# Weight parts, turns and sums in another order in a two-block transformer kernel on one core

## The chip, the cores and the metric

One Trainium2 chip, one of its cores. Work runs on five engines with instruction streams of their own: TensorE (PE, matrix products, with its weight loads as PEld), VectorE (DVE), ScalarE (ACT), GpSimd (POOL) and SyncE (SP); POOL and SP here mostly issue DMAs. The metric is the device time of one execution in microseconds (us), lower is better.

## The reference

Everything is fp32, batch 1, 1024 positions, width 1024, with a context of 256 rows beside them (1280 rows, ten chunks of 128).

```python
def reference(...):
    x = first_block(x, c, ctx, c_ctx, ...)     # two layers
    return second_block(x, p, positions, ...)

# first_block, layer 0: modulation from silu(c) @ w_mod, then
hx = rmsnorm(x, g_pre) * (1 + scale) + shift             # and the same of ctx
ux = hx @ ab_w_in                                        # q, k, v, o, z of 4 heads, pool, gates
qk = short_conv(...)                                     # 3 taps
h  = mlstm_chunkwise(forward) + reversed mlstm_chunkwise # 4 heads, chunks of 128, state C (256x256)
y  = [head_rmsnorm(h*o) * silu(z), multiscale_pool(u) * silu(z)] @ ab_w_out
# layer 1: window attention with context keys and a sink

# second_block
z = rms_norm(h, norm_mix) @ w_in
o_gla  = gla_mixer(...)                                  # 4 heads, chunks of 64
lam = exp(sum(lam_q1*lam_k1)) - exp(sum(lam_q2*lam_k2)) + lam_init
# diff_attention, each of 8 blocks of 128 queries and 4 heads, keys up to the block's end:
pr = softmax(where(mask, q @ k.T, -1e30))                # two maps, m = 0 and 1
o_diff = (pr[0] - lam * pr[1]) @ v
o_diff = rms_norm(o_diff, norm_g) * (1 - lam_init)
h = h + concat(o_gla, o_diff) @ w_out
h = h + (gelu(conv(rms_norm(h) @ w_up)) ...) @ w_down    # feed-forward
gate = sigmoid(rms_norm(h, norm_ple) @ w_ple_gate)
h = h + gate * (p @ w_ple_proj)
return rms_norm(h, norm_final)
```

## The kernel before, in words

The kernel is one program of hand-ordered parts that run behind each other: first stage (0 to about 67 us: modulation vectors, norm, gate product), the four recurrent heads, the pool, the output projection, layer 1, then the second block with its gated linear attention (gla), differential attention, output projection, feed-forward (up, down) and the last part (ple). There is no scheduler: each engine runs its instructions in the order in which the code issues them, and waits on semaphores for the others.

**Products in three passes.** Each fp32 operand is split into a rounded high part and a rest, and three products (high-high, high-low, low-high) are summed. Weights come by DMA into `W`; ACT copies the high part of half an item to `W_rounded` (`split_hi`, line 403) and DVE subtracts to get the rest (`split_lo`, line 412). `split_lo(v, key, n, of)` does the n-th of `of` equal pieces of one half; the semaphore that PE waits for moves with the last piece. Activations are split likewise (`HT_rounded`, `HT_lo`).

**First stage.** w_mod comes as four slices of 512 columns, each in two halves of 1 MB (line 706). PE multiplies a slice by the vectors (`MB`, line 454), DVE copies the 98 rows out (`mod_rows`, 888), PE turns them into columns (`MT`, `TR`, 461), DVE takes them (`mod_cols`, 893) and forms `amul` (902). `value(k)` is the modulated, turned activation of part k, `low(k)` (line 923) its rest. The gate product (`GT`, line 775) comes next on PE.

**Heads.** For head h, PE makes two 128-column units q, k (`G`, line 1195, three row ranges each), then 20 recurrent steps with the state update (`CC`, line 1180; DVE adds it to `c_state`, line 1384). DVE finishes each chunk of output. `turn_y` (PE `X`, line 1104) transposes a finished chunk and `copy_turned_y` (ACT, 1113) copies it out; the last four chunks of a head are done within the next head's first unit (`late`). `X` has one slot for a chunk, which ACT frees. In step 10 of the 20, DVE also makes the rest of the first weight half of the next head.

**Pool.** Projection (`G`, line 2204), window sums (2334), means (2347, 2348) and the weight rest `wlo` on DVE; `prev.done` is a wait for the stored y of the last head; `prev.turn` and `copy_late` are the last head's late chunks.

**Differential attention** (`S` scores, line 3289; `TP` turned weights, 3299; `O`, 3308). Item j is query block j // 4 and head j % 4. PE makes both score maps into `S[:, m, 0:kw]`, DVE adds the mask and takes the negated maximum (`neg_max`, 3407), ACT exponentiates (3349), DVE combines the two maps with lam (`second_share`, 3415, and 3416), PE turns (in step j+2), ACT copies (3357), PE multiplies by v. Before scores j it waits until DVE has read both maps of j-1 (`s_nm >= 2 j`). Between these, `turn_gla` turns one of eight gla chunks into the second bank of `S` and ACT and DVE split it (`z_lo_gla`, 3431). The lam vectors and the norm's gain are loaded from SP (3253, 3256).

**Down projection.** `add(r)` (DVE, 2626) adds a finished row block to the residual; this code is shared by several projections and has variants `gated` and not.

**Last part.** For each of eight row blocks: gate product (`G`, 3807), relu-like cut (ACT 3840), exp, ln, exp (3844 to 3846), the product p @ w_ple_proj (`PP`, 3789), DVE multiply and add (3862, 3865), ACT square with its root (3849, 483, 484), DVE scale (3873), and POOL's store (3765).

## Time and profile before

| | us |
|---|---|
| median of 3 runs | 3405.12 (3401.29 to 3410.22) |
| the profiled execution, its own time | 3408.22 |
| its span | 3406.4 |
| PE busy in it | 3296.8 (97%) |
| DVE busy | 1765.3 (52%) |
| ACT busy | 1510.5 (44%) |
| POOL busy | 110.6 (3%) |

The span is the time from the first to the last recorded instruction; the execution's own time is 1.8 us longer. Busy is the time in which an engine had at least one instruction at work. The mean granted clock of TensorE is 0.988 of full speed. DMA moved 308.38 MB at a mean of 91 GB/s.

### The profile page before, as it was taken

Reading aid. Unit: us, or ns where it says so; the run is one execution under the profiler, and the core shown is the slowest. Engines: PE = TensorE matmul, PEld = TensorE weight load, DVE = VectorE, ACT = ScalarE, POOL = GpSimd, SP = SyncE. Lnnn points to the kernel's source line nnn. Section 1 sums busy time; section 2 is a strip of 40 time slices with the busy share of each in tenths; the row PEclk is TensorE's granted clock in tenths of the full one; section 3 lists DMA queues with packets and bytes.
Section 4 is the critical chain, followed back from the end, with each engine's and each line's share of the span. In section 5 each row is a group of like instructions: output and inputs, shape, how many; then the busy total and the mean of one; then the engine's idle time right before and its main releaser. Section 6 shows DMA issues by size and latency. Waiting matters only on the chain. (4 is left out here: it accounts for less than half of the span.)

```text
span 3406.4 us, 42773 instructions
## 1 busy us (share of the span) xinstructions
PE 3296.8 (97%) x17536; PEld 2664.9 (78%) x17536; DVE 1765.3 (52%) x2736; ACT 1510.5 (44%) x2411; POOL 110.6 (3%) x240
## 2 busy tenths in 40 slices
PE   7999999999999999999999999998999999999997
PEld 5988889797777777887887777775778888878775
DVE  6544444444344467532886644359556544444544
ACT  5343434434224345215786534228435444433445
POOL 2000000000000000001000000000000000000000
PEclk8999999999999999999999999999999999999999
DMA  5202011111333556122301711010331111134553
GB/s 203 70 1 81 29 54 55 53 56 38 141 134 105 190 207 247 56 50 71 91 2 38 195 53 50 26 54 1 130 118 50 50 50 43 44 130 161 179 185 130
DMA packets 187442, 308.38 MB, mean 91 GB/s; under 512 B 28507, under 2 KB 122560, under 8 KB 187120
## 3 DMA queue, kind: packets, MB, share of 16 engines
q1 hardware_dynamic: 165392, 227.60, 20.8%
q0 software_dynamic: 20784, 77.98, 6.5%
q8 instruction: 139, 2.28, 0.3%
q14 instruction: 55, 0.45, 0.0%
q10 hardware_dynamic: 1072, 0.07, 0.0%
HBM read 269.87 MB, written 35.75 MB: 90 GB/s over the span
## 5 line engine op out<-in xcount | busy, mean ns | idle before, releaser
L412 DVE TENSOR_TENSOR W_rounded<-W,W_rounded 128x2048 fp32r<-128x2048 f32 (+1 forms) x172 | 348.9, 2029 | 469.5 <-ACT W_rounded L403 465.7
L403 ACT ACTIVATE W_rounded<-W 128x2048 fp32r<-128x2048 f32 (+1 forms) x172 | 292.5, 1701 | 398.2 <-DMA W<-in_w_down 97.0
L3587 PE MATMUL G<-HT_rounded,W_rounded 128*128 128x512 f32 x1584 | 452.8, 393 | 0.0
L3587 PEld LDWEIGHTS G<-HT_rounded,W_rounded 128*128 128x128 f32 x1584 | 298.3, 188 | 68.4
L2551 PE MATMUL G<-W_rounded,r_y_rounded 128*128 128x512 f32 x960 | 229.7, 400 | 6.1 <-DVE r_y_rounded L2657 4.7
L2551 PE MATMUL G<-W_rounded,x_hi 128*128 128x512 f32 x704 | 222.1, 397 | 3.6 <-DVE act_turned_rounded L2657 3.3
L2551 PEld LDWEIGHTS G<-W_rounded,r_y_rounded 128*128 128x128 f32 x960 | 181.0, 190 | 51.7 <-DVE W_rounded L412 5.7
L2204 PE MATMUL G<-HT_rounded,W_rounded 128*128 128x512 f32 (+1 forms) x768 | 210.1, 358 | 3.7 <-DVE W_rounded L412 3.7
L1151 PE MATMUL G<-W_rounded,HT_rounded 128*128 128x512 f32 x640 | 213.6, 415 | 0.0
L3587 PE MATMUL G<-HT_lo_ffn,W_rounded 128*128 128x512 f32 x528 | 208.5, 395 | 0.0
L1195 PE MATMUL G<-HT_rounded,W_rounded 128*128 128x512 f32 (+1 forms) x768 | 205.7, 354 | 1.0 <-PEq L652 1.0
L2874 PE MATMUL G<-W_rounded,HT_rounded 128*128 128x512 f32 x640 | 203.1, 399 | 0.0
L2204 PEld LDWEIGHTS G<-HT_rounded,W_rounded 128*128 128x128 f32 x768 | 138.0, 190 | 29.1 <-DVE W_rounded L412 4.6
L2551 PEld LDWEIGHTS G<-W_rounded,x_hi 128*128 128x128 f32 x704 | 132.6, 189 | 35.4 <-DVE W_rounded L412 4.3
L1195 PEld LDWEIGHTS G<-HT_rounded,W_rounded 128*128 128x128 f32 x768 | 136.1, 188 | 22.6 <-issue 1.2
L2874 PEld LDWEIGHTS G<-W_rounded,HT_rounded 128*128 128x128 f32 x640 | 118.4, 188 | 28.2 <-issue 2.0
L2551 PE MATMUL G<-W_rounded,act_turned_rounded 128*128 128x512 f32 x352 | 140.1, 398 | 0.0
L1151 PEld LDWEIGHTS G<-W_rounded,HT_rounded 128*128 128x128 f32 x640 | 120.2, 188 | 25.2
L2204 PE MATMUL G<-HT_lo,W_rounded 128*128 128x512 f32 (+1 forms) x384 | 137.4, 358 | 0.0
L1195 PE MATMUL G<-HT_lo,W_rounded 128*128 128x512 f32 (+1 forms) x384 | 136.4, 355 | 0.0
L1650 PE MATMUL G<-W_rounded,HT_rounded 128*128 128x512 f32 x416 | 131.6, 397 | 0.0
L2874 PE MATMUL G<-W_rounded,o_turned_lo 128*128 128x512 f32 x320 | 126.1, 394 | 0.0
(479 smaller groups left out, 6468.9 us busy)
## 6 DMA issues: line engine op xcount, KB each, us to landing
W<-in_w_down SPq DMA_DIRECT2D x33, 1024.0 KB, 4.9
W<-in_ab_w_out SPq DMA_DIRECT2D x32, 1024.0 KB, 5.5
W<-in_w_up SPq DMA_DIRECT2D x44, 512.0 KB, 5.0
W<-in_ab_w_in SPq DMA_DIRECT2D x20, 1024.0 KB, 8.7
W<-in_w_mod SPq DMA_DIRECT2D x8, 2048.0 KB, 8.1
x_rows<-r_xt POOLq DMA_DIRECT2D x32, 512.0 KB, 5.5
W<-in_c_w_out SPq DMA_DIRECT2D x24, 512.0 KB, 7.0
r_xt<-x_rows POOLq DMA_DIRECT2D x24, 512.0 KB, 5.1
```

The source lines that it names most:

```text
L403: ins = a.activation(self.half(key, True)[:, at], self.half(key, False, False)[:, at], ACT.Copy)
L412: ins = v.tensor_tensor(self.half(key, False)[:, at], self.half(key, False, False)[:, at], self.half(key, True)[:, at].bitcast(F32), ALU.s ...
L1151: ins = pe.matmul(G[:, K.par(key), :], x[y][:, 4 * kh + k, r * P:(r + 1) * P], wv[z][:, k, :], start=(kh == 0 and k == 0 and (y, z) == SPL ...
L1195: ins = pe.matmul(G[:, K.par(key), 0:n], wv[y][:, k, cc], x[z][:, k, c0:c0 + n], start=(k == 0 and (y, z) == SPLIT_PASSES[0]), stop=(k == ...
L1650: ins = pe.matmul(bank(key), x[y][:, 4 * kh + k, r * P:(r + 1) * P], w[z][:, k, :], start=(kh == 0 and k == 0 and (y, z) == SPLIT_PASSES[0 ...
L2204: ins = pe.matmul(bank(key, n), w[y][:, k, cc], x[z][:, k, c0:c0 + n], start=(k == 0 and (y, z) == SPLIT_PASSES[0]), stop=(k == KT - 1 and ...
L2551: ins = pe.matmul(slot(r)[:, n * 512:(n + 1) * 512], x[y], w[z][:, k, n * 512:(n + 1) * 512], start=(kk == 0 and k == 0 and (y, z) == SPLI ...
L2874: ins = pe.matmul(bank(key), x[y][:, 4 * kh + k, r * P:(r + 1) * P], w[z][:, k, :], start=first, stop=last)
L3587: ins = pe.matmul(bank(("up", j, half))[:, rc * 512:rc * 512 + 512], w[a][:, k, c], x[b][:, 2 * rc:2 * rc + 2, :], start=(k == 0 and a == ...
```

## The change

Seven places are edited; nothing is computed otherwise than before but for one DVE instruction that has another form.

1. First stage: the halves of w_mod are divided otherwise between the queues of SP (before four, now three) and POOL (before four, now five, both halves of slice 1 among them); DVE copies `mod_rows(3)` before `low(2)`, and `low(3)` to `low(7)` come after the values, the weight rest last.
2. Heads: the four late turns, two after row range 0 and two after range 1 of the first unit instead of four behind the unit. In the pool stage likewise.
3. Heads: the rest of the next head's first half in four quarters, in steps 11 to 14.
4. Pool: `wlo(1)` ahead of `prev.done`.
5. Projections without a gate: all `add` ahead of the step's split, and the following part's second split one step later.
6. Differential attention: scores 2 to 15 alternate between the two banks of `S`; gla turns go to the second bank of `TP` in one slot; lam vectors by POOL; `second_share` with one pointer scalar.
7. End: gate of the last row blocks straight behind each cut; the last product goes to a free slot of `G`; the last row block in halves, its store too, from SP.

```diff
-            for j in range(4):
+            for j in (0, 2, 3):
                 load_mod(sp, j, 0)
...
-            for j in range(4):
+            load_mod(g, 0, 1)
+            for half in range(2):
+                load_mod(g, 1, half)
+            for j in (2, 3):
                 load_mod(g, j, 1)
...
             mod_rows(2)
+            mod_rows(3)
             low(2)
-            mod_rows(3)
             mod_cols(2)
-            low(3)
             mod_cols(3)
             shifts(4)
             value(4)
             value(6)
+            for k in range(3, KT):
+                low(k)
             K.split_lo(v, ("qk", 0, 0))
-            for k in range(4, KT):
-                low(k)
...
-                if ct == 0 and h >= 1:
-                    for n in late:
-                        turn_y(pe, h - 1, n)
+                    if h >= 1 and ct == 0 and rc < 2:
+                        for n in late[2 * rc:2 * rc + 2]:
+                            turn_y(pe, h - 1, n)
...
-                if s == 10:
-                    K.split_lo(v, ("qk", h + 1, 0) if h + 1 < H else ("p", 0, 0))
+                if 11 <= s < 15:
+                    K.split_lo(v, ("qk", h + 1, 0) if h + 1 < H else ("p", 0, 0), s - 11, 4)
...
                 if gi == ct == 0:
+                    wlo(1)
                     prev.done(v)
...
-            if s == len(steps) and following:
+            if not gated:
+                for r in ended(s):
+                    add(r)
+            if s == len(steps) + int(not gated) and following:
                 K.split_lo(v, following[1])
...
-    gla_steps = [1, 3, 5, 7, 9, 11, 13, 14]
+    gla_steps = [1, 3, 5, 7, 9, 11, 13, 15]
...
+    def s_at(j):
+        return 512 * ((j + 1) % 2) if 2 <= j < 16 else 0
...
-            if j >= 1:
+            if j == 2:
+                mix.taken(pe)
+            elif 3 <= j < 16:
+                pe.wait_ge(s_nm, 2 * j - 2)
+            elif j >= 1:
                 pe.wait_ge(s_nm, 2 * j)
...
         def turn_gla(r):
-            if r >= 2:
-                pe.wait_ge(s_gl, r - 1)
+            if r >= 1:
+                pe.wait_ge(s_gl, r)
             for m in range(4):
-                ins = pe.transpose(S[:, r % 2, 512 + m * P:512 + (m + 1) * P], K.Zg[:, r, m * P:(m + 1) * P],
+                ins = pe.transpose(TP[:, 512 + m * P:512 + (m + 1) * P], K.Zg[:, r, m * P:(m + 1) * P],
...
-            ch.link(v.tensor_scalar(cw[:, j:j + 1], sm[:, j, 0:1], rc[:, j, 1:2], lam[:, 3:4], ALU.mult, ALU.mult))
+            ch.link(v.scalar_tensor_tensor(out=cw[:, j:j + 1], in0=sm[:, j, 0:1], scalar=lam[:, 3:4], in1=rc[:, j, 1:2],
+                                           op0=ALU.mult, op1=ALU.mult))
...
+    def product(r):
+        return G[:, (r + 1) % 3, :] if r == XT - 1 else PP[:, :]
...
-            if r:
+            if r == XT - 1:
+                pe.wait_ge(s_gread, r - 1)
+            elif r:
                 pe.wait_ge(s_pp, r)
...
+                    if s == len(steps):
+                        gate(r)
...
-            for r in due(s, 2):
+            for r in [] if s == len(steps) else [XT - 3, XT - 2] if s == len(steps) + 2 else due(s, 2):
```

What stands in each engine's row is shown at three places.

DVE in the first stage, before. The rows go from `low(0)` to the first `amul` of the second group; `HT_lo` is `low`, `mod_rows` and `modc` the copies of rows and columns.

```order
L923 TENSOR_TENSOR HT_lo<-h_value,HT_rounded 128x1280 x2
L888 COPY mod_rows<-MB 98x512
L923 TENSOR_TENSOR HT_lo<-h_value,HT_rounded 128x1280
L888 COPY mod_rows<-MB 98x512
L893 COPY modc<-MT 128x8
L923 TENSOR_TENSOR HT_lo<-h_value,HT_rounded 128x1280
L893 COPY modc<-TR_30 128x8
L899 TENSOR_TENSOR modc<-modc,cols 128x8 x2
L902 SCALAR_TENSOR_TENSOR amul<-modc,cols 128x4 x2
```

The same place after the change.

```order
L926 TENSOR_TENSOR HT_lo<-h_value,HT_rounded 128x1280 x2
L891 COPY mod_rows<-MB 98x512 x2
L926 TENSOR_TENSOR HT_lo<-h_value,HT_rounded 128x1280
L896 COPY modc<-MT 128x8
L896 COPY modc<-TR_30 128x8
L902 TENSOR_TENSOR modc<-modc,cols 128x8 x2
L905 SCALAR_TENSOR_TENSOR amul<-modc,cols 128x4 x2
```

The second copy of `mod_rows` has moved ahead of the third `low`, and the fourth `low` has left this stretch for the place behind the values.

DVE in the first head from step 9 on, before. `W_rounded` is the rest of the next head's first weight half; each `c_state` row begins the work of a step.

```order
L1369 TENSOR_TENSOR qk_conv<-qk_conv,raw 128x2x128
L412 TENSOR_TENSOR W_rounded<-W,W_rounded 128x2048
L1384 SCALAR_TENSOR_TENSOR c_state<-c_state,decay_all,CC 128x514
L1389 TENSOR_TENSOR den<-N,colg 128x1
L1390 SCALAR_TENSOR_TENSOR den<-N,den 128x1
L1393 RECIPROCAL den<-den 128x1
L1395 TENSOR_SCALAR h_rows<-N,den 128x256
L1369 TENSOR_TENSOR qk_conv<-qk_conv,raw 128x2x128
L1407 TENSOR_TENSOR qk_conv<-G,qk_conv 128x256
L1384 SCALAR_TENSOR_TENSOR c_state<-c_state,decay_all,CC 128x514
```

The same engine after the change, from the end of step 10 on.

```order
L1371 TENSOR_TENSOR qk_conv<-qk_conv,raw 128x2x128
L1409 TENSOR_TENSOR qk_conv<-G,qk_conv 128x256
L412 TENSOR_TENSOR W_rounded<-W,W_rounded 128x512
L1386 SCALAR_TENSOR_TENSOR c_state<-c_state,decay_all,CC 128x514
L1391 TENSOR_TENSOR den<-N,colg 128x1
L1392 SCALAR_TENSOR_TENSOR den<-N,den 128x1
L1395 RECIPROCAL den<-den 128x1
L1400 SCALAR_TENSOR_TENSOR h_rows<-N,den,h_rows 128x256
L1371 TENSOR_TENSOR qk_conv<-qk_conv,raw 128x2x128
L1415 TENSOR_TENSOR h_rows<-h_rows,qk_conv 128x256
L412 TENSOR_TENSOR W_rounded<-W,W_rounded 128x512
L1386 SCALAR_TENSOR_TENSOR c_state<-c_state,decay_all,CC 128x514
```

The one instruction of 2048 columns has become pieces of 512, one ahead of each of four `c_state` rows, beginning a step later.

ACT at the end of the kernel, before: `act_turned<-G` is the cut of row blocks 6 and 7, the rows with `x_ss` the square and its root.

```order
L3840 ACTIVATE act_turned<-G,cut 128x1024 x2
L3849 ACTIVATE act_turned,x_ss<-act_turned 128x1024
L483 ACTIVATE x_ss<-x_ss,eps 128x1
L484 ACTIVATE x_ss<-x_ss 128x1
L3844 ACTIVATE act_turned<-act_turned,cut 128x1024
L3845 ACTIVATE act_turned<-act_turned,one 128x1024
L3846 ACTIVATE act_turned<-act_turned 128x1024
L3844 ACTIVATE act_turned<-act_turned,cut 128x1024
L3845 ACTIVATE act_turned<-act_turned,one 128x1024
L3846 ACTIVATE act_turned<-act_turned 128x1024
```

The same after the change.

```order
L3873 ACTIVATE act_turned<-G,cut 128x1024
L3856 ACTIVATE act_turned<-act_turned,cut 128x1024
L3857 ACTIVATE act_turned<-act_turned,one 128x1024
L3858 ACTIVATE act_turned<-act_turned 128x1024
L3873 ACTIVATE act_turned<-G,cut 128x1024
L3856 ACTIVATE act_turned<-act_turned,cut 128x1024
L3857 ACTIVATE act_turned<-act_turned,one 128x1024
L3858 ACTIVATE act_turned<-act_turned 128x1024
L3881 ACTIVATE act_turned,x_ss<-act_turned 128x1024
L483 ACTIVATE x_ss<-x_ss,eps 128x1
```

The three gate passes of block 6 now stand ahead of the cut of block 7, and the square of block 5 behind both gates.

## Rows read from the trace of the kernel before

**Rows 1.** The profile page: busy time and share by engine

```profile
PE 3296.8 (97%) x17536; PEld 2664.9 (78%) x17536; DVE 1765.3 (52%) x2736; ACT 1510.5 (44%) x2411; POOL 110.6 (3%) x240
```

**Rows 2.** Waits of PE, whole span: total us, times, longest us

```profile
PE S L3289 <- DVE neg_max L3407: 7.4, 13, 2.6
PE X L1104 <- ACT qk_conv L1113: 7.2, 8, 1.2
PE CC L1180 <- DVE c_state L1384: 6.3, 4, 1.6
...
PE TP L3299 <- ACT HT L3357: 5.7, 5, 2.2
...
PE G L2204 <- DVE W_rounded L412: 3.7, 1, 3.7
...
PE G L3807 <- DVE r_xt L2626: 2.1, 1, 2.1
...
PE G L2551 <- DVE r_xt L2626: 0.3, 1, 0.3
```

**Rows 3.** DMA queues from 20 to 25 us: packets, MB, share

```profile
q0 software_dynamic: 328, 1.28, 67.2%
q1 hardware_dynamic: 332, 0.65, 35.9%
```

**Rows 4.** Timeline of PE, first stage: start, us, instruction, idle before

```profile
33.69 1.90 PE L454 MATMUL MB<-W,c_cols 128*2 128x512 f32 x16 [1.50 <-DMA W<-in_w_mod]
...
47.83 1.79 PE L461 MATMUL TR<-pick,mod_rows 98*128 98x2 f32 x8 [1.63 <-DVE mod_rows L888]
```

**Rows 5.** Timeline of DVE, first stage

```profile
33.70 1.23 DVE L950 TENSOR_TENSOR w_gate_parts<-w_gate,w_gate_parts 128x1024 fp32r<-128x1024 f32 x1 [0.87 <-ACT w_gate_parts L831]
...
44.40 0.68 DVE L888 COPY mod_rows<-MB 98x512 f32<-98x512 f32 x1
45.68 1.49 DVE L923 TENSOR_TENSOR HT_lo<-h_value,HT_rounded 128x1280 fp32r<-128x1280 f32 x1 [0.59 <-ACT HT_rounded L845]
47.09 0.68 DVE L888 COPY mod_rows<-MB 98x512 f32<-98x512 f32 x1
```

**Rows 6.** Timeline of DVE, first head

```profile
220.27 2.29 DVE L412 TENSOR_TENSOR W_rounded<-W,W_rounded 128x2048 fp32r<-128x2048 f32 x1 [5.42 <-ACT W_rounded L403]
...
237.18 0.75 DVE L1384 SCALAR_TENSOR_TENSOR c_state<-c_state,decay_all,CC 128x514 f32<-128x514 f32 x1 [1.68 <-PE CC L1180]
```

**Rows 7.** Timeline of DVE, pool stage

```profile
869.11 2.29 DVE L412 TENSOR_TENSOR W_rounded<-W,W_rounded 128x2048 fp32r<-128x2048 f32 x1
```

**Rows 8.** Timeline of DVE, down projection

```profile
3263.31 2.35 DVE L2626 TENSOR_TENSOR r_xt<-G,r_xt 128x1024 f32<-128x1024 f32 x2
```

**Rows 9.** Stretches of the differential attention: busy us by engine, PEclk

```profile
2290.00:2300.00 10.00, 6.98 (x34) 4.62 (x34) 7.26 (x39) 5.95 (x27) 0.00 (x0) 0.66 0.12 33
...
2340.00:2370.00 30.00, 27.58 (x189) 19.69 (x190) 28.80 (x73) 24.66 (x62) 0.00 (x0) 1.00 0.01 2
```

**Rows 10.** Timeline of DVE, start of the differential attention

```profile
2291.14 0.23 DVE L3450 CUSTOM_DVE_ANT_0 lam_prod<-lam_vecs 128x64 f32<-128x64 f32 x1 [3.16 <-DMA lam_vecs<-in_lam_k]
```

**Rows 11.** Waits of VectorE from 2286 to 2404: total us, times, longest us

```profile
DVE HT L3407 <- PE S L3289: 6.9, 10, 1.5
```

**Rows 12.** Timeline of ACT, end of the kernel

```profile
3376.57 1.12 ACT L3840 ACTIVATE act_turned<-G,cut 128x1024 f32<-128x1024 f32 x1 [7.48 <-PE G L3807]
...
3381.97 1.13 ACT L3844 ACTIVATE act_turned<-act_turned,cut 128x1024 f32<-128x1024 f32 x1
...
3385.27 1.13 ACT L3844 ACTIVATE act_turned<-act_turned,cut 128x1024 f32<-128x1024 f32 x1
```

**Rows 13.** Timeline of PE, end

```profile
3379.15 3.60 PE L3789 MATMUL PP<-act_turned,p_turned 128*128 128x512 f32 x8
3386.67 5.13 PE L3789 MATMUL PP<-act_turned,p_turned 128*128 128x512 f32 x8 [3.93 <-DVE act_turned L3862]
```

**Rows 14.** Timeline of DVE, end

```profile
3396.23 1.28 DVE L3873 SCALAR_TENSOR_TENSOR act_turned<-act_turned,x_ss 128x1024 f32<-128x1024 f32 x1 [0.64 <-issue]
```

More of the change, by code:

```diff
@@ L2663, in vector @@
                     tail[2](v, 0)
-            for r in ended(s)[1:] if per >= 8 else []:
+            for r in ended(s)[1:] if gated and per >= 8 else []:
                 add(r)
@@ L3762, in gpsimd @@
             load(r)
-        for r in range(XT):
+        for r in range(XT - 1):
             g.wait_ge(s_ob, r + 1)
```

104 lines of the change are left out of this document (59 added, 45 removed).

## The prediction

> **What bounds the kernel now.** I read the page's busy line first. TensorE is busy for 3296.8 us of a span of 3406.4 [rows 1], so 109.6 us are all that an order of work can give back, and only what it takes out of TensorE's idle time counts; VectorE and ScalarE are half idle over the whole. The second view is the list of TensorE's waits [rows 2]: each names the instruction that was late, how often, and for how long. The third is the timeline around each of these, which tells what stood ahead of the late instruction on its engine. The last block of the kernel is another matter: there the chain of single instructions behind the last gate product sets the end.
>
> The sum is made against the profiled execution: 3408.2 us, its span and 1.8 us around it. The median of the runs shown is 3405.1, 3.1 less, and the forecast is moved down by these 3.1.
>
> **First stage: 2.3 us.** TensorE's turn of the last rows began at 47.83 after 1.63 us of idling for the copy of `mod_rows` [rows 4]. That copy stood at 47.09 behind a rest of 1.49 us that nothing needed yet [rows 5]. With the two copies adjacent it follows the one at 44.40, at 45.1, and the wait of 1.63 goes. The rests of parts 3 to 7 are made later, but the gate product takes the parts one after another; I put nothing on it, and have no row that shows the room. The other half is the queues. From 20 to 25 us both moved as many packets (328 and 332), but POOL's are twice as large: 1.28 MB against 0.65 [rows 3]. A half slice of 1.05 MB so takes 4.1 us on POOL's and 8.1 on SP's. Slice 1 needed the second half in SP's row and its sums waited 1.50 us, to 33.69 [rows 4]. On POOL's queue it is the third half, 3.15 MB and 12.3 us from the start instead of 2.1 MB and 16.2, so 2 to 4 us earlier. But its copy needs VectorE, which has the parts of the gate weights until 34.93 [rows 5]; before, the copy came at about 35.6. That leaves 0.7. Bounds: 0.7 (only slice 1 helps, or a later part is late by what the copies give) to 4.0 (both in full).
>
> The Trainium skill, DMA: Bandwidth & Descriptors, section "Queues, rings and completion order", says that each DMA engine takes turns between queues by packet, and the equal packet counts agree with it. If the engines shared by bytes instead, slice 1's third megabyte on POOL's queue would come at the pace of SP's; that is a rival below.
>
> **Heads, late turns: 2.2 us.** TensorE waited eight times for the one slot that ScalarE frees, 7.2 us in all and 1.2 at most [rows 2]. Four of them, at the heads' ends, are of the longest kind, 1.24 each and 5.0 in all, and stay; the other four, the remaining 2.2 us (0.55 each), lie behind the first unit, where four turns stand together. Two behind each of two row ranges meet a free slot after the first pair. Bounds: 2.2, and 1 us of loss, if ScalarE's copies make the next evacuation late.
>
> **Heads, weight rest: 6.3 us.** In step 10 of each head VectorE does 2.29 us on the next weights [rows 6], and the state behind it is late: TensorE waits 1.6, four times, 6.3 in all [rows 2]. In quarters a piece is an estimated 0.57 us (2.29 / 4), ahead of a state update each in steps 11 to 14, where VectorE itself idles 1.68 us for TensorE ahead of the update [rows 6]. All four fit. The pieces end about four steps later than before, still before the head's end, and the next head's first product is far behind them. Bounds: 4 (each piece costs a tenth of a us on the state) to 6.3.
>
> **Pool: 3.7 us.** The rest of 2.29 us at 869.11 [rows 7] is what TensorE waits for, 3.7 us, once [rows 2]. It stands behind window sums that wait for a stored y and for other data. Moved ahead of that wait it is ready before TensorE asks. The window sums begin 2.29 us later at most, in a stretch in which they wait for the DMA anyway. Bounds: 0, if VectorE is then the next to be late, to 3.7.
>
> **Down projection: 2.4 us.** Two waits for the residual's sum, 2.1 and 0.3 us [rows 2]. The two sums take 2.35 us at 3263.31 [rows 8] behind a rest of as much again; in the other order they come first. The rest is then 2.35 us later, and the following part's second rest a step later; they are needed one item of products later, and I cost them at nothing. Bounds: 1.5 (one of these rests is late in its turn) to 2.4.
>
> **Differential attention: 4.0 us, the term I trust least.** TensorE waits 7.4 us for the negated maximum (13 times) and 5.7 us for ScalarE's copy of the turned weights [rows 2], and idles 3.0 us of 10 in the stretch from 2290 [rows 9]. Two score buffers let scores j+1 start while the maximum of j is taken. But in the stretch from 2340 VectorE is busy for 28.80 of 30 us against TensorE's 27.58 [rows 9]: the second buffer lets TensorE run ahead, and VectorE sets the pace. So only what VectorE idles can come back: 3.16 us at the start for the lam vectors [rows 10], which now go out from POOL and not from SP's queue, and part of the 6.9 us for which it waits for scores, in ten pieces [rows 11]; the first pieces are those of items that depend on each other in any order, so I count up to 5.2 of them. Against it stands the single slot of the gla turns, which makes TensorE wait for VectorE's read seven times more, at an estimated 0.1 to 0.4 us each. The one-pointer form of `second_share` takes up to 0.1 us from each of 32 instructions, all on VectorE's path; with that as part I take 1.5 us from lam, 1.1 from the last gla step that no longer stands ahead of the scores of item 16, and 1.4 from the rest. Bounds: 3 us of loss (the single slot costs most, the buffers give nothing) to 9 of gain (8.4 of VectorE's idle and a little of the instruction).
>
> **End: 5.4 us.** Before, both cuts come first and the gate of block 6 starts at 3381.97 and the one of block 7 at 3385.27 [rows 12], 3.30 us per gate. The product of block 7 can't begin before block 6's is read, at 3386.67, and takes 5.13 us at a lowered clock instead of 3.60 [rows 13]. From its end at 3391.80 to that of the last scale at 3397.51 [rows 14] are 5.7 us: three full passes of VectorE (1.28 each) and 1.9 of square and root. After: the cut of block 6 ends at 3377.69 [rows 12], its gate at 3381.0, the cut of block 7 at 3382.1, its gate at 3385.4. The product of block 7 goes to a slot of its own right behind block 6's, which ran from 3379.15 for 3.60 [rows 13]; so it ends at 3386.3, its first half at 3384.5. Four half passes (0.65 each) from 3385.4 end at 3388.0, square and root at 3389.9, while VectorE scales blocks 5 and 6 until 3390.7; two half scales end at 3392.0. That is 5.5 us before 3397.51. Three row blocks are stored close together instead of two, for which I take off 0.1. Bounds: 4 to 6.
>
> **Sum.** 2.3 + 2.2 + 6.3 + 3.7 + 2.4 + 4.0 + 5.4 = 26.3, so 3408.2 - 26.3 = 3381.9 for the profiled execution and 3378.8 for the median, as 3379. With all the lower bounds the gain is 0.7 - 1 + 4 + 0 + 1.5 - 3 + 4 = 6.2 and with the upper ones 4.0 + 2.2 + 6.3 + 3.7 + 2.4 + 9 + 6 = 33.6.
>
> **Rivals.**
> *The differential attention gives all that VectorE idles.* The buffers and lam bring 8.4 us and not 4. For it: thirteen waits for the maximum go at once. Against it: VectorE's share near 96%. Time: 3379 - 4.4 = 3374.6. The Trainium skill, TensorE: Matmul & The Clock Gate, section "HAM oscillation — how this bites in real kernels", says that repeated gaps in TensorE's work lower its clock; by that rule, filled gaps would also lift the clock of 0.66 in the stretch from 2290, which the row shows beside idling of 3 us in 10. That by itself would be a mechanism of this kernel: 6.98 us of busy time [rows 9], a part of it at the lower of the two levels, would shrink by 2 to 3 us, which is again about 3376.
> *Gains given back.* Behind a wait that goes stands the next: the pool gives 0, the late turns 0, the differential attention 0. For it: each of these was a wait with another engine's instruction close behind. Time: 3379 + 3.7 + 2.2 + 4.0 = 3388.9.
> *Queues share by bytes.* Slice 1 then arrives later than before, as POOL's third megabyte instead of SP's second: half as much again, about 3 us, and TensorE waits for it. Against it: [rows 3]. Time: 3382.
> *The change doesn't do what it says.* The waits that are named are moved, not removed; only first stage and end give their 7.7 us. Time: 3379 + 18.6 = 3397.6, within what can't be told from no change.
> *Slower.* TensorE falls to the 1.2 GHz level in the differential attention. For it: 0.66 in the stretch from 2290 [rows 9], in bursts with waits between. The stretch from 2340 holds 27.58 us of TensorE's work at full clock; at the lower level it would be 27.6 us more, which eats the sum, and from some 37 us of such work the kernel is slower by what can be measured. With 45 us of it: 3379 + 4 + 45 = 3428. Against it: busy shares there rise with the change, not fall.
>
> **How the numbers follow.** Forecast 0.55, all of VectorE's idle 0.15, gains given back 0.15, bytes 0.05, nothing of the waits 0.07, slower 0.03. The likeliest is 3379. The range, 3368 to 3392, takes in the first four, the bounds of their terms and the 4.5 us by which runs of one kernel differ; what is left out is the last two and the far ends. A difference of 0.3%, 10.2 us, is about what a measurement of this kernel can tell from none. Faster by more: the first four, 0.90. Within: 0.07. Slower: 0.03.
>
> **What would show it.** Gone from TensorE's waits: `c_state` (6.3), `W_rounded` at `G` of the pool (3.7), `r_xt` (2.4), and `mod_rows` in the first stage; the slot `X` falls from 7.2 to 5.0. `PP` no longer waits, and the last scale ends about 9 us before the span's end, as before (3397.5 and 3406.4), and that 26 us earlier. In the differential attention the wait for the maximum falls from 7.4 to 4 or less and VectorE's idle at lam from 3.16 to under 2. The largest errors are to be looked for there, and in a stretch of lower clock.

## The result and the profile after

The changed kernel took 3373.11 us (median of 4 runs, 3369.95 to 3381.77) against 3406.86 (4 runs, 3401.29 to 3410.22): ratio 0.9897, 95% interval 0.9876 to 0.9917. The forecast was 3379 with a range of 3368 to 3392. A second comparison in more rounds gave 3377.22 against 3403.75, ratio 0.9916 (0.9899 to 0.9932). Over all runs on record it is nine runs of the changed kernel with a mean of 3376.5 and 30 of the one before with a mean of 3406.3: 29.8 us, against 26.3 forecast.

The profiled execution has a span of 3371.1 us, 35.3 less than before. These are the busy and the clock line of its page.

```profile
PE 3282.1 (97%) x17536; PEld 2661.5 (79%) x17536; DVE 1765.7 (52%) x2751; ACT 1509.0 (45%) x2411; POOL 112.8 (3%) x245
...
PEclk9999999999999999999999999999999999999999
```

TensorE is busy 14.7 us less than before [rows 1], although it makes the same 17536 products. Only 20.6 us of the 35.3 are idle time that went. That is the first thing to explain. The list of TensorE's waits answers to [rows 2] (total us, times, longest).

```profile
PE TP L3313 <- ACT HT L3369: 7.5, 6, 2.3
...
PE X L1106 <- ACT qk_conv L1115: 4.9, 4, 1.2
PE TP L3313 <- DVE HT L3429: 4.6, 6, 1.6
...
PE S L3303 <- DVE neg_max L3419: 2.5, 6, 0.9
...
PE MB L454 <- DMA W<-in_w_mod: 2.4, 2, 2.0
```

`c_state`, `W_rounded` in the pool, `r_xt` and `mod_rows` are gone from it (`mod_rows` in this trace alone, see below), and the slot `X` is down from 7.2 to 4.9 us, four times. The wait for the maximum fell from 7.4 to 2.5, but both waits for the turned weights grew: 5.7 to 7.5, and 2.6 to 4.6.

Both traces hold the same matmuls, so the start of the same one can be compared in both. The difference, read at the stages' ends, is what each stage gave. A second trace of each kernel (both are among the experiments) tells which of these numbers belong to the change: the first stage, the pool and the stages that weren't touched differ between two traces of one kernel by up to 6.5 us each.

| stage | forecast | profiled executions | what is in it |
|---|---|---|---|
| first stage | 2.3 | 5.2 | 2.8 until the gate product, 2.4 within it |
| heads, late turns | 2.2 with the pool's | 4.1 with the pool's | 1.02 to 1.04 at each of 4 boundaries |
| heads, weight rest | 6.3 | 7.3 | 1.8 in each head |
| pool | 3.7 | 6.5 | 3.7 the wait, 2.8 in the products behind it |
| from the pool's end to the differential attention (not touched) | 0 | -3.4 | |
| differential attention | 4.0 | 2.2 | |
| up (not touched) | 0 | 2.6 | |
| down | 2.4 | 5.3 | 1.7 of it at its start |
| end | 5.4 | 5.5 | |

**First stage.** PE first, then DVE (answering to [rows 4] and [rows 5]).

```profile
32.90 1.90 PE L454 MATMUL MB<-W,c_cols 128*2 128x512 f32 x16 [0.38 <-DMA W<-in_w_mod]
...
45.75 1.03 PE L461 MATMUL TR<-pick,mod_rows 98*128 98x2 f32 x8
46.64 0.47 PE L778 MATMUL GT<-HT_rounded,w_gate_parts 128*128 128x512 f32 x1
```

```profile
43.93 0.69 DVE L891 COPY mod_rows<-MB 98x512 f32<-98x512 f32 x1
44.80 0.69 DVE L891 COPY mod_rows<-MB 98x512 f32<-98x512 f32 x1 [0.18 <-PE MB L454]
45.41 1.48 DVE L926 TENSOR_TENSOR HT_lo<-h_value,HT_rounded 128x1280 fp32r<-128x1280 f32 x1
```

Slice 1's sums start at 32.90 instead of 33.69, with a wait of 0.38 us instead of 1.50. The two copies of rows stand together, the turn `TR` waits for nothing, and the gate product starts at 46.64; before, `TR` started at 47.83 and took 1.79. The two queues move equal packets as before, which answers to [rows 3]:

```profile
q0 software_dynamic: 329, 1.28, 67.2%
q1 hardware_dynamic: 329, 0.64, 35.6%
```

The other 2.4 us are clock in this pair of traces. These are rows of the view by stretches from 50 to 60 us, before and after (busy us and instructions of PE, PEld, DVE, ACT and POOL, then the granted clock).

```profile
50.00:60.00 10.00, 10.00 (x41) 8.27 (x40) 9.82 (x13) 8.23 (x8) 0.00 (x0) 0.76 0.19 60
```

```profile
50.00:60.00 10.00, 10.00 (x54) 8.46 (x53) 9.05 (x7) 6.66 (x8) 0.00 (x0) 1.00 0.19 59
```

TensorE is busy all the time in both, but makes 54 products instead of 41 in it, at a granted clock of 1.00 (2.4 GHz) instead of 0.76 (a part at 1.2 GHz).

Neither number of this pair stands for the kernels. In the changed kernel's second trace the gate product starts at 48.93 and the stage ends at 66.2 us, where the one before has 67.2 and in its second trace 66.3. TensorE waits for the copy of rows again, now in the turn `MT`:

```profile
PE MT L461 <- DVE mod_rows L891: 3.0, 1, 3.0
```

Over the three traces with the first stage as before, the gate product starts at 49.3 to 51.0 us, 49.9 in the mean; over the eight with the changed one at 46.3 to 48.9, 47.7 in the mean. That is 2.3 us, the forecast. From there to the stage's end it is 17.1 us in the mean of the three and 16.9 in that of the eight, so that the clock's 2.4 us are chance.

**Late turns.** PE before, at the first boundary, and after.

```profile
273.39 0.60 PE L1104 MATMUL X<-ident,h_rows 128*128 128x128 f32 x4
274.54 0.96 PE L1104 MATMUL X<-ident,h_rows 128*128 128x128 f32 x4 [0.56 <-ACT qk_conv L1113]
275.25 0.48 PE L1195 MATMUL G<-HT_rounded,W_rounded 128*128 128x512 f32 x1
```

```profile
257.92 0.60 PE L1106 MATMUL X<-ident,h_rows 128*128 128x128 f32 x4
258.27 0.48 PE L1197 MATMUL G<-HT_rounded,W_rounded 128*128 128x512 f32 x1
...
263.88 0.60 PE L1106 MATMUL X<-ident,h_rows 128*128 128x128 f32 x4
264.24 0.37 PE L1197 MATMUL G<-HT_rounded,W_rounded 128*128 128x256 f32 x1
```

Before, it is 1.86 us from the first turn to the next product: the profile calls 0.56 of it idle, but the second group of turns is 0.96 long where 0.60 is usual, so more waiting is inside it. After, each pair costs 0.35. The difference is 1.15, twice what the wait's row says, and 1.02 to 1.04 of it are left at the end of the unit.

**Weight rest.** DVE in the first head after, answering to [rows 6].

```profile
228.37 0.68 DVE L412 TENSOR_TENSOR W_rounded<-W,W_rounded 128x512 fp32r<-128x512 f32 x1
230.04 0.75 DVE L1386 SCALAR_TENSOR_TENSOR c_state<-c_state,decay_all,CC 128x514 f32<-128x514 f32 x1 [0.98 <-PE CC L1182]
```

A quarter is 0.68 us, not 0.57, and VectorE still idles 0.98 for TensorE ahead of the update.

**Pool.** DVE, answering to [rows 7]: the rest now stands ahead of the window sums and waits only for its high part.

```profile
837.77 2.29 DVE L412 TENSOR_TENSOR W_rounded<-W,W_rounded 128x2048 fp32r<-128x2048 f32 x1 [14.01 <-ACT W_rounded L403]
839.98 1.52 DVE L2338 TENSOR_TENSOR window_sums<-raw 128x1311 f32<-128x1311 f32 x1
```

**Differential attention.** DVE at its start, answering to [rows 10], and two stretches that answer to [rows 9].

```profile
2268.14 0.22 DVE L3463 CUSTOM_DVE_ANT_0 lam_prod<-lam_vecs 128x64 f32<-128x64 f32 x1
...
2270.88 0.16 DVE L3471 TENSOR_TENSOR lam<-lam 128x1 f32<-128x1 f32 x1 [1.57 <-ACT lam L3400]
```

```profile
2270.00:2280.00 10.00, 7.34 (x38) 4.65 (x38) 7.10 (x35) 6.89 (x30) 0.00 (x0) 0.83 0.01 2
2320.00:2350.00 30.00, 27.96 (x197) 20.43 (x196) 28.74 (x73) 24.41 (x62) 0.00 (x0) 1.00 0.01 2
```

The vectors are there, but the lam value itself waits 1.57 us for ScalarE's exponentials. In the stretch of 30 us VectorE is busy 28.74 us as before (28.80). And its wait for the scores, of which the prediction counted on up to 5.2 us, has not fallen from 6.9 us [rows 11] but risen:

```profile
DVE HT L3419 <- PE S L3303: 7.7, 10, 2.6
```

**End.** ACT, PE and DVE, answering to [rows 12], [rows 13] and [rows 14].

```profile
3347.88 1.15 ACT L3856 ACTIVATE act_turned<-act_turned,cut 128x1024 f32<-128x1024 f32 x1
...
3352.34 1.15 ACT L3856 ACTIVATE act_turned<-act_turned,cut 128x1024 f32<-128x1024 f32 x1
```

```profile
3349.31 3.60 PE L3813 MATMUL PP<-act_turned,p_turned 128*128 128x512 f32 x8
3352.74 3.60 PE L3813 MATMUL G<-act_turned,p_turned 128*128 128x512 f32 x8
```

```profile
3355.79 0.69 DVE L3896 TENSOR_TENSOR act_turned<-act_turned,G 128x512 f32<-128x512 f32 x1 [0.30 <-ACT act_turned L3858]
...
3358.45 3.80 DVE L3910 SCALAR_TENSOR_TENSOR act_turned<-act_turned,x_ss 128x1024 f32<-128x1024 f32 x4
```

The gates are 4.46 us apart, the cut of block 7 between them. The product of block 7 runs behind that of block 6, 3.60 us each. From the last gate product's end to the last scale's end it is 12.78 us, and was 18.20: 5.42 less, as forecast. To the end of the span it is 27.1 to 28.7 us in the four traces with the old end and 21.3 to 21.7 in the nine with the new one.

### The profile page after: what moved, and what is told of

Its sections match the earlier page's. It is cut to its first block and busy times, and to the rows that moved or that the text cites. A ratio compares the mean times of both kernels' runs of the same rounds, so it can differ in the third digit from the quotient of the medians.

```text
span 3371.1 us, 42790 instructions
## 1 busy us (share of the span) xinstructions
PE 3282.1 (97%) x17536; PEld 2661.5 (79%) x17536; DVE 1765.7 (52%) x2751; ACT 1509.0 (45%) x2411; POOL 112.8 (3%) x245
## 5 line engine op out<-in xcount | busy, mean ns | idle before, releaser
L412 DVE TENSOR_TENSOR W_rounded<-W,W_rounded 128x2048 fp32r<-128x2048 f32 (+2 forms) x184 | 350.8, 1907 | 458.6 <-ACT W_rounded L403 454.5
L1386 DVE SCALAR_TENSOR_TENSOR c_state<-c_state,decay_all,CC 128x514 f32<-128x514 f32 x64 | 48.0, 750 | 156.6 <-PE CC L1182 156.6
```

The source lines that it names most:

```text
L412: ins = v.tensor_tensor(self.half(key, False)[:, at], self.half(key, False, False)[:, at], self.half(key, True)[:, at].bitcast(F32), ALU.s ...
L1386: v.scalar_tensor_tensor(out=cs[:, d, :, :], in0=cs[:, d, :, :], scalar=dec[:, d, h, c:c + 1], in1=prod, op0=ALU.mult, op1=ALU.add).then_i ...
```

## The experiments

Stage times below are read as in the table above, at the same matmuls of two traces. The stretch at 881 us in the expectations is counted as the clock's records count; in the span's time it is at 871. "The lower level" is the granted clock of 0.5 (1.2 GHz). Items of the differential attention are counted from the end of their last score product. Where no number of runs is given, the kernel was executed once, so that its total time tells little; its stage times count.

**The differential attention as before.** The edit takes part 6 out of the changed kernel.

```diff
-        return 512 * ((j + 1) % 2) if 2 <= j < 16 else 0    # and all else of part 6
+            if j >= 1:
+                pe.wait_ge(s_nm, 2 * j)
```

> The changed kernel with the differential attention as before (two score maps in one buffer, gla turns in two slots, lam vectors from SP, two pointer scalars). Theory A, the prediction's: the differential attention is worth 4.0 us, so this kernel is 4.0 slower than the changed one, about 3377 us. Theory B, from the trace of the changed kernel, in which TensorE idles 16.7 us in that stage instead of 19.3 and is busy 2.5 us longer: VectorE sets the pace there and the part is worth 1 to 1.5 us, so about 3374.5 us. From TensorE's first score matmul to the last turn of the stage A expects 4.0 us more than in the changed kernel, B 1 to 1.5. Both expect all other stages as in the changed kernel.

Measured: 3381.45 us (4 runs, 3379.54 to 3391.52), ratio to the kernel before 0.9932 (0.9913 to 0.9952). The stage is 2.1 us longer than in the changed kernel (127.45 against 125.39 us from the first score product to the last turn), between A's and B's numbers. The rest of the difference in the profiled executions lies in stages that are the same in both kernels, 3.0 us in the first stage and 2.5 in the up projection behind the differential attention (see "One score buffer").

**Part 6 alone**, in the kernel before.

> The kernel before with the new differential attention alone. Theory A, the prediction's: 4.0 us faster than before. Theory B, VectorE sets the pace: 1 to 1.5 us faster, which no total time can tell from nothing; in the stage TensorE's wait for the maximum is 2 to 3 us instead of 7.4, its waits for the two other engines' work on the turned weights 12 instead of 8.3. In the pool stage the clock stretch at 881 us is there as before.

Measured: 3403.73 us (10 runs) against 3405.63 (13), ratio 0.9993 (0.9983 to 1.0003): nothing that the total can tell. The stage is 125.28 us long and was 127.57: 2.3. TensorE's waits changed as in the changed kernel (2.5, 7.5 and 4.7). For the stage 4.0 was too much and B's 1 to 1.5 too little. The total refutes neither: its interval goes from 1.0 us slower to 5.8 faster.

**Its pieces, in the changed kernel.** Lam from SP again, and in the pool `wlo(1)` behind `prev.done` again:

```diff
     def sync(sp):
-        pass
+        mix.sines(sp)
+        for n, name in enumerate(("lam_q1_2", "lam_k1_2", "lam_q2_2", "lam_k2_2")):
+            sp.dma_start(lv[:, n, :], i[name].to_broadcast([P, 64])).then_inc(s_in, 16)
...
-                    wlo(1)
                     prev.done(v)
```

> The changed kernel with two things undone: the lam vectors and the norm's gain are loaded from SP again, and in the pool stage the weight rest stands behind the wait for y again. Theory A (lam is worth what VectorE idled for it, 1.5 us or more of the stage): the differential attention is 1.5 to 2.2 us longer than in the changed kernel, and VectorE's idle for the vectors is 3 us again. Theory B (TensorE and ScalarE catch up behind it, since the lam value itself waits for ScalarE's exponentials): 0.5 or less. For the pool: the prediction's theory has the wait of 3.7 us for the weight rest back; the rival, from the kernel with the queues, turns and end alone, is that the earlier late turns already bring y 3 us sooner, so that only 0.7 us comes back.

Measured: 3375.58 us. The stage is 1.1 us longer, all of it ahead of item 4 (11.32 us against 10.21, both with 3 us at the lower clock level; the rest is equal to 0.04). Lam is worth 1.1: between the two theories. In the pool the prediction's theory fell; the wait list has 0.9 us, not 3.7.

```profile
PE G L2206 <- DVE W_rounded L412: 0.9, 1, 0.9
```

**Two pointers, and the last row block whole.**

```diff
-            ch.link(v.scalar_tensor_tensor(out=cw[:, j:j + 1], in0=sm[:, j, 0:1], scalar=lam[:, 3:4], in1=rc[:, j, 1:2],
-                                           op0=ALU.mult, op1=ALU.mult))
+            ch.link(v.tensor_scalar(cw[:, j:j + 1], sm[:, j, 0:1], rc[:, j, 1:2], lam[:, 3:4], ALU.mult, ALU.mult))
...
-                halves = [slice(0, 512), slice(512, D)] if r == XT - 1 else [slice(0, D)]
+                halves = [slice(0, D)]
```

> The changed kernel with two things undone: the share of the second map with two pointer scalars again (0.27 instead of 0.22 us, 32 times, all on VectorE), and the last row block whole: one product, full passes of VectorE, one store of 512 KB. If VectorE sets the pace of the differential attention this costs about 1.5 us there (32 times 0.05); if not, nothing. At the end the prediction's working gives 1.3 us longer: the product's second half is late by 0.9 for a full pass, and the last scale is not overlapped with the store of its first half.

Measured: 3378.53 us. In items 16 to 31, which ran at full clock in both, the stage is 0.5 us longer (79.92 against 79.40 us), so the instruction's 0.05 us is passed on by a part only (32 times 0.05 would be 1.6 in the whole stage). At the end the last scale ends 13.04 us behind the last gate product instead of 12.78.

```profile
3362.32 1.22 DVE L3893 TENSOR_TENSOR act_turned<-act_turned,G 128x1024 f32<-128x1024 f32 x1 [0.95 <-PE G L3810]
...
3364.72 3.67 DVE L3907 SCALAR_TENSOR_TENSOR act_turned<-act_turned,x_ss 128x1024 f32<-128x1024 f32 x3
```

Up to the last scale the halves are worth 0.3 us, not 1.3, and to the end of the span nothing: from the last gate product it is 21.4 us with the whole row and 21.7 with the halves. The product of a whole row is waited for 0.95 us, but the passes in halves cost more than half each (0.69 against 1.22), which takes most of it back.

**One score buffer.**

```diff
-        return 512 * ((j + 1) % 2) if 2 <= j < 16 else 0
+        return 0
...
-            elif 3 <= j < 16:
-                pe.wait_ge(s_nm, 2 * j - 2)
```

> The changed kernel with one score buffer: scores j wait for both maxima of j-1, as before the change; gla turns in the single slot and lam vectors from POOL as in the changed kernel. Theory A (the second buffer is what the stage gains by): the stage is 2 us or more longer, the wait for the maximum back at 7 us. Theory B (VectorE and ScalarE set the pace): the wait for the maximum is back at 6 to 7 us, but the waits for the turned weights fall by 3 to 4 us, and the stage is 0 to 1 us longer.

Measured: 3383.49 us for the execution, with a stage 2.0 us longer. But the lower clock level holds 13.7 us of the stage instead of 6.8. In items 12 to 31, where both have the same clock, it is 94.90 us against 94.99: nothing. TensorE's waits (total, times, longest):

```profile
PE TP L3311 <- ACT HT L3367: 6.7, 6, 1.9
...
PE S L3301 <- DVE neg_max L3417: 3.5, 10, 0.9
PE TP L3311 <- DVE HT L3427: 3.4, 3, 1.6
```

The wait for the maximum is 3.5 us and not 7, and the waits for the turned weights are 10.1 instead of 12.1. At equal clock the wait moves from one line to another and the pace stays: theory B. The single slot of the gla turns costs nothing that this run shows either.

But the 2.0 us may be more than chance. These are the rows of the whole stage in the kernel before, in this one and in the changed one (the number behind the counts is the granted clock).

```profile
2286.06:2413.62 127.56, 107.75 (x710) 77.12 (x710) 105.91 (x298) 98.19 (x268) 0.00 (x0) 0.96 0.04 12
```

```profile
2271.79:2399.20 127.41, 111.17 (x710) 79.35 (x710) 104.54 (x298) 98.15 (x268) 0.00 (x0) 0.95 0.03 9
```

```profile
2266.30:2391.69 125.39, 108.02 (x710) 77.63 (x710) 104.53 (x298) 97.80 (x268) 0.00 (x0) 0.97 0.03 9
```

From the first score product to a product of the up projection 286 us behind the stage, all six traces with one score buffer have 17.1 us at the lower level. Of the seven with two buffers six have 10.2 and one has 13.7. The time between these two products is 412.7 to 415.2 us with one buffer and 408.6 to 412.8 with two, and this kernel, which differs from the changed one in nothing else, has 412.7 against 409.3 and 409.6 in the two traces of the latter. So the second buffer seems to be worth some 3 us after all, by the clock and partly behind its own stage. Why the clock follows it isn't shown, and the totals don't settle it: part 6 alone has a mean clock of 0.9895 in its ten runs where the kernel before has 0.9894 in the thirteen beside them, while the changed kernel without part 6 has 0.9895 in four runs against 0.9910 in nine with it.

**The weight pieces on GpSimd.**

```diff
-            if 16 <= j < 24:
-                K.split_lo(v, ("out2", 0, 1), j - 16, 8)
...
+        for n in range(8):
+            K.split_lo(g, ("out2", 0, 1), n, 8)
```

> The changed kernel, but the rest of the next projection's second weight half (8 pieces of 0.42 us in items 16 to 23) is made by GpSimd, which idles, instead of VectorE. Theory A (TensorE's waits set the pace): no change in the stage, 0.3 us or less. Theory B (VectorE sets the pace in the second half of the stage, 28.7 of 30 us busy): the stage is 2.5 to 3.3 us shorter. A rival to both: GpSimd's passes slow VectorE's by a shared port, and the stage gets no shorter or longer.

Measured: 3373.47 us. The pieces take GpSimd 5.97 us, and the wait for the maximum goes to 1.0.

```profile
2303.24 5.97 POOL L412 TENSOR_TENSOR W_rounded<-W,W_rounded 128x256 fp32r<-128x256 f32 x8 [117.66 <-ACT W_rounded L403]
```

```profile
PE S L3305 <- DVE neg_max L3421: 1.0, 2, 0.9
```

Items 16 to 27, which lose 3.3 us of VectorE's work, are 1.3 us shorter (46.37 against 47.70), the stage as a whole 0.9. So VectorE's work is on the path for some four tenths. That the rest is ScalarE's, behind each maximum, is likely and not shown. Neither theory had that number, and A, by which nothing would change, fell. A part of the third, the rival, came true. These are VectorE's share of the second map and its combination while GpSimd is at work, in items 12 to 15:

```profile
2303.44 0.54 DVE L3429 SCALAR_TENSOR_TENSOR second_share<-sums,lam,recip_sums 128x1 f32<-128x1 f32 x1
2304.01 1.19 DVE L3431 SCALAR_TENSOR_TENSOR HT<-HT,second_share 128x512 f32<-128x512 f32 x1
```

They take 0.22 and 0.75 us otherwise, and the next share takes 0.76. That is 1.3 us in three instructions, while VectorE's passes over the scores took 0.69 us as always, and these four items are 0.5 us longer than in the changed kernel (15.9 against 15.4). Whether a shared port is the reason, as the rival has it, no run here shows.

**The orders on VectorE alone**, in the kernel before (parts 3 and 4, and the first stage's order).

> The kernel before with three orders on VectorE alone: the first stage's copies of rows ahead of the rests (queues as before), the weight rest of the next head in four quarters, the pool's weight rest ahead of the wait for y. Theory A, the prediction's (each wait that goes gives its length and no more): 1.6 us in the first stage, 6.3 in the heads (1.6 each), 3.7 in the pool, 11.6 in all. Theory B, from the trace of the changed kernel: a wait that goes ahead of a stretch at the lower clock level takes a part of that stretch with it, so that the first stage gives about 2 us more and the pool about 2.4 more (the products from 871 to 877 us run at full clock), 16 in all.

Measured: 3390.64 us, span 17.6 us shorter. Heads 1.86, 1.82, 1.81 and 1.79, sum 7.3; pool 6.5; first stage 2.8, with the gate product at 47.50 instead of 49.48. That is 16.6 where B has 16 and A 11.6; the last 1.0 lies in stages that the edit doesn't touch. B owes this to the one trace of the kernel before: against its second trace, in which the pool's products run at full clock, the pool gives 3.7 and the first stage 2.0, and that is A for the pool.

**Queues, turns and end alone.**

> The kernel before with the other division of w_mod between the queues (VectorE's order as before), the late turns of the heads two and two, and the new end. Theory A, the prediction's: 0.7 us in the first stage, 0.55 at each of four unit boundaries, 5.4 at the end, 8.3 in all. Theory B, from the trace of the changed kernel: 1.1 at each of the four boundaries, since a part of the wait for the slot stood inside a run of turns that the profile counted as busy, and 5.6 at the end, so 10.5 to 11 in all. The clock stretch at 881 us (1.2 GHz, 6.8 us) is there as before by theory B of the second kernel, since the pool's wait of 3.7 us is.

Measured: 3389.03 us, span 19.2 us shorter. Boundaries 1.06, 1.04, 1.04 and 1.05; end 5.9 (5.42 to the last scale, the rest behind it); first stage 2.5, with the gate product at 47.87. In the pool stage it gained 5.7 us that neither theory had. The wait list has the reason, and so has VectorE's window sum; the first row is this kernel's wait of TensorE, the second its `window_sums`, the third the same in the kernel before.

```profile
PE G L2207 <- DVE W_rounded L412: 0.7, 1, 0.7
```

```profile
849.22 1.52 DVE L2338 TENSOR_TENSOR window_sums<-raw 128x1311 f32<-128x1311 f32 x1 [15.36 <-DMA y_turned<-qk_conv]
```

```profile
858.58 1.53 DVE L2334 TENSOR_TENSOR window_sums<-raw 128x1311 f32<-128x1311 f32 x1 [19.16 <-DMA y_turned<-qk_conv]
```

TensorE's wait is 0.7 us and not 3.7. The window sums start at 849.22 instead of 858.58: 9.4 us earlier, of which 6.6 are what the stages ahead gave. With the late turns in pairs the last y is copied and stored sooner. The two edits remove one and the same wait.

**The changed kernel again.**

> The changed kernel once more, beside the one before, in more rounds. Theory A (the gain is what the orders give, 27 to 28 us, and the rest is chance of the profiled executions): ratio 0.992 and a mean granted clock as that of the runs of before, 0.9893 in thirteen. Theory B (with its waits the change also takes away stretches at the lower clock level): 33 us, ratio 0.990 to 0.991, and a mean granted clock of 0.9905 to 0.991.

Measured: 3377.22 us (5 runs, 3370.33 to 3388.73) against 3403.75 (9), ratio 0.9916 (0.9899 to 0.9932); mean clock 0.9912. Over the nine runs of the changed kernel the mean clock is 0.9910, over the 26 of the one before that have one on record 0.9895. B's clock came true; the time doesn't decide, since the medians are 26.5 us apart and the interval of the ratio holds A's number and B's. 0.0015 of 3400 us are 5.1 us, of which 1.6 lie behind the last gate product, where the lower level holds 14.8 us in the mean of four traces with the old end and 11.6 in that of nine with the new one.

This kernel's profiled execution, at 3388.73 us the longest, lost 6.5 us against the first one at each of two places that the change doesn't touch. At the later, between 1920 and 1970 us, the lower level holds 10.2 us more. At the earlier, about 1270 to 1335 us, it holds 3.4 us more and a weight load is late: ScalarE waits 11.4 us for `in_ab_w_out` at the longest, and 3.9 in the first trace.

**The kernel before again**, for a second trace.

> The kernel before once more, for a second trace of it. Theory B (the change takes stretches of the lower clock level away with its waits): the stretch at 881 us, ahead of which TensorE waits 3.7 us, is there again (it was in both traces without the pool's edits and in none of eight with one of them), and the total of lower-clock time ahead of the last gate product is above 50 us. Theory A (chance): the stretch at 881 may be missing, and the total lies anywhere between 41 and 58 us, as in the kernels with the edits.

Measured: 3404.91 us. These are the rows of the stretch from 870 to 880 us, of the first trace and of the second, and the second's wait ahead of it.

```profile
870.00:880.00 10.00, 8.54 (x25) 6.81 (x26) 6.54 (x5) 1.92 (x1) 0.53 (x1) 0.66 0.86 300
```

```profile
870.00:880.00 10.00, 9.57 (x42) 7.84 (x43) 5.52 (x5) 3.23 (x4) 0.53 (x1) 1.00 0.76 260
```

```profile
PE G L2204 <- DVE W_rounded L412: 3.6, 1, 3.6
```

The wait is there and the stretch at the lower level is not (this trace has none between 53 and 1302 us); the total ahead of the last gate product is 54.6 us, against 68.3 in the first trace and 47.8 in the first of the changed kernel. The tie between that wait and that stretch, theory B, is refuted. What holds is the mean over runs. The pool, from the first product behind the late turns on, takes 148.1 us in the first trace, 145.4 in this one and 141.6 in both of the changed kernel, the last three at full clock: 3.8 us is what the change gives, and not 6.6.

**A version with more.** Three edits on the changed kernel: the fifth late turn joins the others, the last part's third weight half is split ahead of the last row block's rest, and the pieces go to GpSimd as above.

```diff
-    late = [n for n in range(NT) if second_visit[final[n]] + TURN_AFTER >= S]
+    late = [n for n in range(NT) if second_visit[final[n]] + TURN_AFTER >= S - 1]
...
+                        if third and r == nr - 1:
+                            K.split_lo(v, third)
                         B.vec_lo(v, r)
```

> A version meant to beat both kernels: the changed kernel with (1) the fifth late turn of each head moved into the next head's first unit as well, behind its third row range, where it stood behind a wait of 1.24 us for the slot, four times; (2) the third weight half of the last part split into high part and rest ahead of the last row block's own split, where TensorE waited 2.5 us for it; (3) the pieces of the weight rest in the differential attention on GpSimd, as in the run with that edit alone. By the waits of the profile: 5.0 + 2.5 + 0.9 = 8.4 us less than the changed kernel. Rival: the y of the last chunk is stored 2.6 us later and the pool's window sums with it, so that the pool's weight rest is late again and takes back up to 2 us.

Measured: 3370.19 us (4 runs, 3368.13 to 3372.27), ratio to the kernel before 0.9900 (0.9885 to 0.9915), beside 3377.22 of the changed kernel in the same comparison (and 3373.11 in the first). It is the fastest of the study, by 7 of the 8.4 us expected, though the two kernels' runs overlap and so do the intervals of their ratios. The slot's wait and the last part's wait are gone. At the boundary to the pool another stands in its place:

```profile
PE G L2206 <- DVE qk_conv L1409: 1.3, 1, 1.3
```

TensorE's first product there waits 1.3 us for VectorE's gating of the last chunk, which the turn's wait had covered.

## Why the prediction was right, and where its steps were not

- **What bounds the kernel** held: each stage gave what left TensorE's path. But "only what it takes out of TensorE's idle time counts" did not: of 35.3 us in the profiled executions 14.7 came out of busy time. Some of it is waiting inside runs of instructions that the profile joins (the turns), most is clock. The sum left the clock out. In the mean over runs the clock brings 3 to 5 us, in the two profiled executions about 10 (68.3 us at the lower level against 47.8, half of it lost), for the first trace of the kernel before had more such time than any other of the study.
- The total is in part luck. The sum came within 3.5 us of the 29.8 that the runs have in the mean because the errors of its terms partly cancel: 1.9 too little for the late turns, 1.0 for the weight rest, 1.8 too much for the differential attention, and the clock in no term.
- **First stage**: right, 2.3 us in the mean of the traces. The single ones give 2.8, 2.0 for the order alone and 1.6 for the queues alone, but the gate product's starts lie 2.7 us apart in eight traces with the same first stage, so how the two share the gain isn't known.
- **Late turns** were mis-sized: 4.1 and not 2.2, because the row "0.56" was taken for the whole wait.
- **Weight rest**: 7.3 against 6.3, right in its working. The quarters' longer passes cost nothing.
- **Pool**: 3.7 is right as a sum, but not as this edit's. With the late turns moved, the edit itself is worth 0.9 to 1.0. The further 2.8 of the first pair of traces are clock that the second trace of the kernel before doesn't have.
- **Down**: 2.4 forecast. The stretch that holds the larger wait (3250 to 3290 us of the kernel before) gave 2.4 us in the changed kernel and in the one with the differential attention as before, and 0.1, -0.4 and -1.4 in the three without part 5, the last with 3.4 us more at the lower level; the rest of the 5.3 is clock at the stage's start (1.7) and 1.2 in between, of which 0.6 to 1.0 came in two kernels without the part too.
- **Differential attention** failed in size: 2.2 against 4.0. Lam was taken at 1.5 and is 1.1, since the value waits for ScalarE next. The last gla step and "the rest" (2.5) don't show: the 6.9 us for which VectorE waits for scores became 7.7, so nothing of the 5.2 that were counted came back. The two pointers give about 0.5 in the second half. What remains, some 0.6, is no more than the 3.4 us less at the lower level can give. The argument that VectorE sets the pace was right, and should have been carried through to a smaller number. What it left out is the 2.5 us that the up projection behind gained (see "One score buffer").
- **End**: 5.4 against 5.42 to the last scale. The working held step by step, except that its halves were thought worth more; the gates of blocks 6 and 7 are 4.46 us apart where it had 4.4.

Of the rivals, "gains given back" came true in the differential attention alone, and there by half. That VectorE's idle all comes back is refuted by the wait that rose, but the second mechanism named there, a clock that filled gaps lift, came in part: in the stage 6.8 us at the lower level instead of 10.2. Queues by bytes, a change without effect, and a fall to the lower level in the differential attention didn't come.

**Open:** why the changed kernel has a higher mean clock. Less idling may be the cause, but the one tie that was tested, at 871 us, didn't hold, and the one that all thirteen traces bear out, with the second score buffer, wasn't tested by more traces of one kernel with a single buffer.

## What to carry to other kernels

Where one engine is busy 97% of the time, read its waits one by one and the instruction ahead of each late one; most of this gain is small pieces of another engine's work, put a few places later. Price a wait by the time from the instruction before to the one after it, not by its idle row alone, and ask whether two edits remove the same wait. Where two engines are both near 90% in a stage, a second buffer moves the third one's wait to another line at equal clock; look all the same at the clock in the stage and behind it. And take a second trace of both kernels before a stage's number is believed: here the first pair said 5.2 us for the first stage and 6.5 for the pool, and more traces 2.3 and 3.8.

## What the runs showed of the hardware

- TensorE's granted clock falls to the lower level for 3 to 10 us at 9 to 14 places of the span ahead of the last gate product, 41 to 68 us in all. Some places recur in all thirteen traces (the first stage, the differential attention, and near 1285, 1600 and 1835 us of the changed kernel); others come and go between executions of the same kernel, as the one at 871 us did. Between two traces of one kernel the sum differed by 13.7 us (68.3 and 54.6) and by 10.2 (47.8 and 58.0), half of which is time, and it hid or doubled several terms in single traces.
- VectorE's 128 x 1 product with one pointer scalar and a tensor took 0.220 us, with two pointer scalars 0.273.
- The subtraction of a 128 x 256 fp32 piece took 0.42 us on VectorE and 0.78 on GpSimd (0.72 seven times and 1.17 once). Beside it three VectorE instructions took 0.54, 0.76 and 1.19 us instead of 0.22, 0.22 and 0.75, while VectorE's passes over the scores kept their 0.69.
- With a last row block of 512 KB stored whole, the span ended 21.4 us behind the last gate product, with two halves 21.3 to 21.7 us.
